# Alternating the two streams' rows in the last block, and issuing five weight splits earlier in the first

## The chip, the cores and the metric

The kernel runs on one core of one Trainium2 chip. The metric is the device time of one execution in microseconds. Engines are named as in the profile: PE is TensorE (matmuls), PEld its weight loads, DVE is VectorE, ACT ScalarE, POOL GpSimd, SP the engine that issues most DMAs.

## The reference

Two layers of a streaming encoder, applied to a prompt of 2048 frames and to a sample of 32 frames, each with its own conditioning vector and (for the sample) its own caches.

```python
h = rms_norm(x, norm_g) * (1.0 + scale) + shift          # scale, shift, gate from c @ w_ada + b_ada
# layer 0
q, k, v, g_a, u, g_s = split(h @ w_in_even)
o_a = sink_attention(rope(q), rope(k), v)                # 64-frame chunks, 2 chunks back
o_s = ssm_branch(u)                                      # complex diagonal recurrence, gelu, GLU
x = x + gate * (concat(o_a * silu(g_a), o_s * silu(g_s)) @ w_out_even)
# layer 1
b_g, c_g, hv, g_c = split(h @ w_in_odd)
x = x + gate * ((silu(g_c) * b_g * short_conv(c_g * hv)) @ w_out_odd)
y = rms_norm(x, final_g)
```

Returned are y of both, the new keys and values, the recurrence's last state and the last rows of the convolution's input. Everything is float32.

## The kernel before

Features lie on the 128 partitions, frames along the free axis; a row k (0 to 7) is one group of 128 of the 1024 features. The prompt is done in four blocks of 512 frames. The sample is a second stream, which goes along with the prompt in block 4 only: `streams_of(b)` gives `[(prompt, b)]` for blocks 1 to 3 and `[(prompt, 4), (sample, 1)]` for the last. Every engine runs its own hand-written program (`run_block`), in order, and the engines meet at counting semaphores, one for each kind of event of a stream: `S.wait(engine, block, event, k)` waits for the k-th such event.

A float32 product is made of three matmuls on parts: each activation and each weight is split into a rounded high part and the rest. `project` (L768) is one 1024 x 128 projection: for each row k, hi x hi, hi x lo, lo x hi. In the last block the two streams stand side by side in `hh_wide` and `hl_wide` (32 + 512 columns), and a row is 6 matmuls of 272 columns on each weight chunk (L789). With `ready`, `project` waits at row k for that row's event of every stream. It is called so for the pair c0, hv0 (event `h1`) and for the pair out1_0, out1_1 (event `g1`).

The activations' parts are made so:
- Norm 1, ahead of c0: PE puts the inverse roots into a bank (L822). DVE's `scale` (L1590) writes x times the root and a weight for row k into one of two buffers (L1598). ACT's `shift` (L1106) adds a bias and rounds (the high part, L1116). DVE makes the low part of row k-1 (L1604) in the same call of `scale`. `scale` needs the low part of row k-2, whose buffer it overwrites.
- Ahead of out1: POOL makes the last gated row (L1427), ACT's `round_mixed` rounds (L1130), DVE's `split_mixed` (L1627) subtracts (L1631).
- Norm 2, at the end: DVE's `output` (L1609) writes a row of y (L1612). When all eight rows of the prompt are there SP stores them, then the sample's, then ten small outputs.

The weights' parts are made in block 1 only, and stored for the later blocks, which load both parts with one DMA. In block 1 SP loads a raw chunk into a ring of two (L590), ACT rounds it into its slot of five (`split_hi`, L504, instruction L514), POOL subtracts (`split_lo`, L516, instruction L523), SP stores both. `load_raw(n)` waits until chunk n-2 is split, and `split_hi` until the slot's former chunk has been used and stored. Projections run in the order k, v, q0, q1, (transposes of u, the recurrence's input products x), q2, q3, ga0 to ga3, y (which takes four pairs loaded from `ssm_scratch`, L616), scores, gs0.

In block 1 the engines do between q0 and ga3, in this order:
- ACT: round q0 and q1; `swap` q0 and q1 (L1139, four copies that exchange halves for the rotary embedding); round q2, q3, ga0, ga1; swap q2; round ga2; swap q3; round ga3.
- DVE: `cos_part` of q0 and q1 (L1650, each waits for its swap); copy the transposed u (uT, L1782); products of x with cos and sin (L1663); `recurrence` (small adds L1677, two scans L1680, then products and h, L1684 to L1692); `cos_part` of q2 and q3.
- POOL: low halves of q0 and q1; sums of the input products (L1370, L1372); low halves of q2 and q3; two products of the scans (L1380, L1381); low half of ga0; h (L1390, L1394); low half of ga1; `rotate` q0 (L1351, L1354), `rotate` q1, low half of ga2, `rotate` q2, low half of ga3, `rotate` q3. The swap of q2 waits for the rotation of q0, the swap of q3 for that of q1.

Of the kernel before, what the change touches and what calls it, by code (L numbers as in the profile page):

```python
# [15 lines left out]
KT = D // P  # L16
# [32 lines left out]
SPLIT = [c for c in DENSE if not c.startswith("glu")]  # L49
# [248 lines left out]
def encoder(nc, vec, bc, d_skip, consts, mask, rope, xs, w_ada, w_dense, caches, outs):  # L298
    y_out, k_out, v_out, hre_out, him_out, conv_out = outs
    ctx = ExitStack()  # L300
    with ctx:
# [742 lines left out]
        def _(act):  # L1044
# [134 lines left out]
            def run_block(blk, streams, last=False):  # L1179
# [18 lines left out]
                for i in range(2):  # L1198
                    for S, b in streams(blk):
                        swap(S, b, f"q{i}", 1 + i)  # L1200
                for name, i in (("q2", None), ("q3", None), ("ga0", None), ("ga1", 2), ("ga2", 3), ("ga3", None)):
                    hi(name)
                    for S, b in streams(blk):
                        if i:
                            swap(S, b, f"q{i}", 1 + i)
# [59 lines left out]
                for S, b in streams(blk):  # L1265
                    shift(S, b, 1)
# [23 lines left out]
                for S, b in streams(blk):  # L1290
                    for k in range(KT):
                        round_mixed(S, b, 1, k)
# [25 lines left out]
        def _(pool):  # L1318
# [37 lines left out]
            def run_block(blk, streams, last=False):  # L1356
# [6 lines left out]
                lo("q0")  # L1363
                lo("q1")
# [9 lines left out]
                lo("q2")  # L1374
                lo("q3")
                for S, b in streams(blk):
# [6 lines left out]
                    if S.prompt:  # L1383
                        lo("ga0")
                        if blk == 1:
                            pool.wait_ge(split, SPLIT.index("ga0") + 1)
# [9 lines left out]
                lo("ga1")  # L1396
# [57 lines left out]
        def _(dve):  # L1454
# [160 lines left out]
            def norms(streams, l):  # L1615
                for S, b in streams:
                    mean(S, b, l)
                for S, b in streams:
                    diagonal(S, b, l)
                for S, b in streams:  # L1620
                    for k in range(KT + 1):
                        if l < 2:
                            scale(S, b, l, k)
                        elif k < KT:
                            output(S, b, k)

            def split_mixed(S, b, l, ks):  # L1627

                for k in ks:
                    S.wait(dve, b, f"g_hi{l}", k + 1)  # L1630
                    dve.tensor_tensor(S.hl[:, k, :], S.g[:, k, :], S.hh[:, k, :].bitcast(F32), ALU.subtract)\  # L1631
                        .then_inc(S.sem[f"g{l}"], 1)
# [124 lines left out]
            def run_block(blk, streams, last=False):  # L1757
# [124 lines left out]
                for S, b in streams(blk):  # L1882
                    split_mixed(S, b, 1, range(8))
# [144 lines left out]
```

## Time and profile before

| | us |
|---|---|
| median of 3 runs | 2185.78 (2183.31 to 2186.01) |
| the profiled execution | 2184.55 |
| its span | 2182.8 |
| PE busy | 2053.6 (94%) |
| PEld busy | 1638.3 (75%) |
| DVE busy | 801.2 (37%) |
| ACT busy | 496.6 (23%) |
| POOL busy | 442.2 (20%) |
| mean granted clock of TensorE | 0.958 of full speed |

Busy times are sums over the engine's instructions in one profiled execution. The span runs from its first to its last instruction. The chain that ended last tells which of them set the end; a wait is idle time of an engine just before an instruction, put down to what released it. Block 1 lies from about 130 to 640 us, the last block from about 1600 to the end.

### The profile page before, as it was taken

Reading aid. Unit: us, or ns where it says so; the run is one execution under the profiler, and the core shown is the slowest. Engines: PE = TensorE matmul, PEld = TensorE weight load, DVE = VectorE, ACT = ScalarE, POOL = GpSimd, SP = SyncE. Lnnn points to the kernel's source line nnn. Section 1 sums busy time; section 2 is a strip of 40 time slices with the busy share of each in tenths; the row PEclk is TensorE's granted clock in tenths of the full one; section 3 lists DMA queues with packets and bytes.
Section 4 is the critical chain, followed back from the end, with each engine's and each line's share of the span. In section 5 each row is a group of like instructions: output and inputs, shape, how many; then the busy total and the mean of one; then the engine's idle time right before and its main releaser. Section 6 shows DMA issues by size and latency. Waiting matters only on the chain.

```text
span 2182.8 us, 27958 instructions
## 1 busy us (share of the span) xinstructions
PE 2053.6 (94%) x11418; PEld 1638.3 (75%) x11434; DVE 801.2 (37%) x1502; ACT 496.6 (23%) x1047; POOL 442.2 (20%) x312
## 2 busy tenths in 40 slices
PE   8887899899999999999999999999999999799986
PEld 2256666688888857788887757888799876699986
DVE  7535272423443551312235543212425162322222
ACT  1232343322221431100121531000211442200010
POOL 0024514455431301001114001010104100100001
PEclk9988999999999999999999999999998999899998
DMA  8886735697778524555466414655474321345432
GB/s 283 309 240 231 263 152 172 242 316 273 259 291 264 188 87 173 193 189 188 175 198 243 173 62 169 233 191 187 156 235 148 127 78 69 125 155 175 176 145 72
DMA packets 86275, 415.00 MB, mean 190 GB/s; under 512 B 12404, under 2 KB 13460, under 8 KB 51892
## 3 DMA queue, kind: packets, MB, share of 16 engines
q1 hardware_dynamic: 79360, 396.37, 51.3%
q10 hardware_dynamic: 6788, 16.84, 2.6%
q8 instruction: 91, 1.49, 0.3%
q14 instruction: 36, 0.29, 0.0%
HBM read 323.51 MB, written 86.33 MB: 188 GB/s over the span
## 4 chain that ended last, share of the span: by engine, by line
PE 87%; DVE 4%; DMA 3%; POOL 2%; issue 2%; ACT 1%; SPq 0%; DVEq 0%; ACTq 0%; POOLq 0%
PE banks L762 17%; PE banks L760 17%; PE banks L761 17%; PE banks L789 16%; PE banks L1004 5%; PE banks L704 3%; PE banks L962 1%; PE banks L943 1%; PE banks L963 1%; PE banks L881 1%; PE banks L839 1%; DMA ring<-in_ada 1%; PE banks L869 1%; PE banks L812 1%; PE banks L822 1%
## 5 line engine op out<-in xcount | busy, mean ns | idle before, releaser
L760 PE MATMUL banks<-hh,pair 128*128 128x512 f32 x1464 | 584.5, 399 | 24.9 <-POOL pair L523 14.5
L762 PE MATMUL banks<-hh,pair 128*128 128x512 f32 x1464 | 584.8, 399 | 0.0
L761 PE MATMUL banks<-hl,pair 128*128 128x512 f32 x1464 | 577.4, 394 | 0.0
L789 PE MATMUL banks<-hh,pair 128*128 128x272 f32 x1952 | 332.9, 292 | 28.9 <-DVE hl L1604 12.7
L760 PEld LDWEIGHTS banks<-hh,pair 128*128 128x128 f32 x1464 | 278.8, 190 | 100.4 <-POOL pair L523 16.6
L761 PEld LDWEIGHTS banks<-hl,pair 128*128 128x128 f32 x1464 | 278.8, 190 | 68.0 <-issue 1.4
L762 PEld LDWEIGHTS banks<-hh,pair 128*128 128x128 f32 x1464 | 278.5, 190 | 61.5
L789 PEld LDWEIGHTS banks<-hh,pair 128*128 128x128 f32 x1952 | 282.4, 193 | 30.4 <-DVE hl L1604 12.8
L789 PE MATMUL banks<-hl,pair 128*128 128x272 f32 x976 | 205.1, 292 | 0.0
L523 POOL TENSOR_TENSOR pair<-ring,pair 128x1024 fp32r<-128x1024 f32 x62 | 152.8, 2467 | 209.2 <-ACT pair L514 209.2
L1339 POOL TENSOR_TENSOR pp_mem<-pp_mem 128x512 f32<-128x512 f32 x48 | 62.1, 1294 | 578.0 <-ACT pp_mem L1104 578.0
L789 PEld LDWEIGHTS banks<-hl,pair 128*128 128x128 f32 x976 | 156.8, 192 | 0.0
L1427 POOL TENSOR_TENSOR p_g<-p_t,pp_mem 128x512 f32<-128x512 f32 x32 | 41.8, 1307 | 551.1 <-DVE p_t L1878 551.1
L1753 DVE SCALAR_TENSOR_TENSOR p_x<-banks,mod,p_x 128x512 f32<-128x512 f32 x64 | 47.4, 750 | 269.6 <-PE banks L762 185.8
L1854 DVE TENSOR_TENSOR pp_mem<-p_sw,banks 128x512 f32<-128x512 f32 x32 | 22.0, 688 | 312.5 <-PE banks L762 223.3
L1004 PE MATMUL banks<-p_uT,pair 128*128 128x512 f32 x256 | 113.4, 602 | 0.0
L1104 ACT ACTIVATE pp_mem<-p_x 128x512 f32<-128x512 f32 x64 | 40.4, 632 | 285.6 <-DVE p_x L1753 285.2
L1139 ACT ACTIVATE p_sw<-banks 32x512 f32<-32x512 f32 x80 | 47.1, 589 | 221.5 <-POOL p_ut L1354 136.7
L760 PE MATMUL banks<-pair,hh 128*128 128x512 f32 (+1 forms) x272 | 93.6, 344 | 2.1 <-DVE hl L1604 2.1
L1004 PEld LDWEIGHTS banks<-p_uT,pair 128*128 128x128 f32 x256 | 48.3, 192 | 59.6 <-issue 54.5
L762 PE MATMUL banks<-pair,hl 128*128 128x512 f32 (+1 forms) x272 | 92.2, 339 | 0.0
L761 PE MATMUL banks<-pair,hh 128*128 128x512 f32 (+1 forms) x272 | 91.9, 338 | 0.0
(294 smaller groups left out, 2300.2 us busy)
## 6 DMA issues: line engine op xcount, KB each, us to landing
pair<-parts_scratch SPq DMA_DIRECT2D x198, 1024.0 KB, 4.8
parts_scratch<-pair SPq DMA_DIRECT2D x66, 1024.0 KB, 7.7
ring<-in_dense SPq DMA_DIRECT2D x62, 512.0 KB, 5.2
pair<-ssm_scratch SPq DMA_DIRECT2D x24, 1024.0 KB, 7.5
ring<-in_ada SPq DMA_DIRECT2D x24, 512.0 KB, 4.7
p_H<-in_ada SPq DMA_DIRECT2D x24, 512.0 KB, 4.7
p_x<-in_x SPq DMA_DIRECT2D x4, 2048.0 KB, 24.7
pair<-glu_scratch SPq DMA_DIRECT2D x8, 1024.0 KB, 5.0
```

The costliest lines, as they stand in the source:

```text
L523: pool.tensor_tensor(lo, raw(n), hi.bitcast(F32), ALU.subtract).then_inc(split, 1)
L704: mm = pe.matmul(psum[2 + j % 2][0:2, :], c_in[:, 2 * (i % 4) + k, :], ada_slots[i % NADASLOT][:, 512 * k:512 * k + 512], start=(i % 4 == ...
L760: pe.matmul(o, ah, bh, start=first, stop=False)
L761: pe.matmul(o, ah, bl, start=False, stop=False)
L762: return pe.matmul(o, al, bh, start=False, stop=last)
L789: mm = pe.matmul(o[n][:, WAT + WCOLS * half:WAT + WCOLS * (half + 1)], x, h[:, k, WCOLS * half:WCOLS * (half + 1)], start=(k == 0 and step ...
L1004: mm = pe.matmul(o, w[:, k, part * P:(part + 1) * P], S.yT[:, k, :], start=(k == 0), stop=(k == 3))
L1104: act.activation(sq[:, k % 2, :], x[:, k, :], ACT.Square).then_inc(S.sem[f"squared{l}"], 1)
L1139: ins = act.activation(S.sw[to:to + 32, n % 2, :], o[fr:fr + 32, 0:S.N], ACT.Copy)
L1339: pool.tensor_tensor(total, before, sq[:, k % 2, :], ALU.add).then_inc(S.sem[f"summed{l}"], 1)
L1427: pool.tensor_tensor(S.g[:, i, :], S.t1[:, i % 2, :], S.yc[:, i % 2, :], ALU.mult)\
L1753: dve.scalar_tensor_tensor(out=S.x[:, i, :], in0=o[:, 0:S.N], scalar=mod[:, l, 16 + i, S.index:S.index + 1], in1=S.x[:, i, :], op0=ALU.mul ...
```

## The change

Three loops over streams are turned inside out for norm 1 and for out1 (ACT and DVE), and with them DVE's loop of norm 2, which is the same function. Where only one stream runs, the order of instructions stays. In block 1 ACT rounds q2 and q3 between the swaps of q0 and q1. POOL makes the low halves of q2, q3 and ga0 right behind q1's, and that of ga1 behind the input sums. POOL's wait for its own split of ga0 goes. No instruction is added or taken away beside that wait; in blocks 2 to 4 the split calls do nothing.

```diff
@@ scalar, run_block
-                for i in range(2):
-                    for S, b in streams(blk):
-                        swap(S, b, f"q{i}", 1 + i)
-                for name, i in (("q2", None), ("q3", None), ("ga0", None), ("ga1", 2), ("ga2", 3), ("ga3", None)):
+                for S, b in streams(blk):
+                    swap(S, b, "q0", 1)
+                hi("q2")
+                hi("q3")
+                for S, b in streams(blk):
+                    swap(S, b, "q1", 2)
+                for name, i in (("ga0", None), ("ga1", 2), ("ga2", 3), ("ga3", None)):
...
-                for S, b in streams(blk):
-                    shift(S, b, 1)
+                for k in range(KT):
+                    for S, b in streams(blk):
+                        shift(S, b, 1, (k,))
...
-                for S, b in streams(blk):
-                    for k in range(KT):
+                for k in range(KT):
+                    for S, b in streams(blk):
                         round_mixed(S, b, 1, k)
@@ gpsimd, run_block
-                lo("q0")
-                lo("q1")
+                for name in ("q0", "q1", "q2", "q3", "ga0"):
+                    lo(name)
...
-                lo("q2")
-                lo("q3")
+                lo("ga1")
...
-                    if S.prompt:
-                        lo("ga0")
-                        if blk == 1:
-                            pool.wait_ge(split, SPLIT.index("ga0") + 1)
...
-                lo("ga1")
@@ vector, norms
-                for S, b in streams:
-                    for k in range(KT + 1):
+                for k in range(KT + 1):
+                    for S, b in streams:
                         if l < 2:
                             scale(S, b, l, k)
@@ vector, run_block
-                for S, b in streams(blk):
-                    split_mixed(S, b, 1, range(8))
+                for k in range(KT):
+                    for S, b in streams(blk):
+                        split_mixed(S, b, 1, (k,))
```

## Rows read from the trace of the kernel before

**Rows 1.** The page's chain that ended last, shares of the span by engine
```profile
PE 87%; DVE 4%; DMA 3%; POOL 2%; issue 2%; ACT 1%; SPq 0%; DVEq 0%; ACTq 0%; POOLq 0%
```

**Rows 2.** PE's waits, whole span: waiting line, releaser, us in total, times, longest
```profile
PE banks L760 <- POOL pair L523: 14.5, 4, 7.5
PE banks L789 <- DVE hl L1604: 12.7, 1, 12.7
...
PE banks L789 <- DVE hl L1631: 7.0, 1, 7.0
...
PE banks L962 <- DMA pair<-ssm_scratch: 3.7, 2, 2.4
```

**Rows 3.** Timeline of DVE, norm 1, last block: start, us, instruction, [idle before, releaser]
```profile
1896.31 0.75 DVE L1598 SCALAR_TENSOR_TENSOR pp_mem<-p_x,gscale,banks 128x512 f32<-128x512 f32 x1
1896.97 0.75 DVE L1604 SCALAR_TENSOR_TENSOR hl<-pp_mem,mod,hh 128x512 fp32r<-128x512 f32 x1
...
1906.76 0.25 DVE L1604 SCALAR_TENSOR_TENSOR hl<-s_im,mod,hh 128x32 fp32r<-128x32 f32 x1 [0.29 <-ACT hh L1116]
```

**Rows 4.** Timeline of DVE, norm 2 (the outputs of both streams)
```profile
2166.28 5.36 DVE L1612 SCALAR_TENSOR_TENSOR p_g<-p_x,vecs,banks 128x512 f32<-128x512 f32 x8 [2.14 <-PE banks L822]
2171.55 1.35 DVE L1612 SCALAR_TENSOR_TENSOR s_g<-s_x,vecs,banks 128x32 f32<-128x32 f32 x8
```

**Rows 5.** Timeline of PE, c0 and hv0; between these rows lie 20 more matmuls
```profile
1907.12 0.79 PE L789 MATMUL banks<-hh,pair 128*128 128x272 f32 x2 [12.74 <-DVE hl L1604]
...
1912.24 0.79 PE L789 MATMUL banks<-hh,pair 128*128 128x272 f32 x4
```

**Rows 6.** The chain in order of time, out1 stage: start, us, what
```profile
2108.82 50.55 PE banks L789 x384
```

**Rows 7.** Timelines of DVE and of POOL ahead of out1
```profile
2102.57 6.04 DVE L1631 TENSOR_TENSOR hl<-p_g,hh 128x512 fp32r<-128x512 f32 x8
...
2102.61 1.78 POOL L1427 TENSOR_TENSOR p_g<-p_t,pp_mem 128x512 f32<-128x512 f32 x1 [22.50 <-DVE p_t L1878]
```

**Rows 8.** The page's group of POOL's gated product: busy us, mean ns, idle before
```profile
L1427 POOL TENSOR_TENSOR p_g<-p_t,pp_mem 128x512 f32<-128x512 f32 x32 | 41.8, 1307 | 551.1 <-DVE p_t L1878 551.1
```

**Rows 9.** Busy time by stretch; behind POOL: PEclk, DMA share, GB/s
```profile
2104.00:2108.00 4.00, 0.00 (x0) 0.00 (x0) 4.00 (x7) 3.13 (x13) 1.06 (x2) 0.88 0.46 193
...
220.00:225.00 5.00, 4.15 (x18) 3.43 (x19) 4.16 (x2) 0.00 (x0) 4.84 (x3) 1.00 0.66 180
```

**Rows 10.** Timeline of ACT, block 1: the swap of q1, the roundings of q2 and q3
```profile
184.38 2.39 ACT L1139 ACTIVATE p_sw<-banks 32x512 f32<-32x512 f32 x4 [3.12 <-PE banks L762]
186.79 1.06 ACT L514 ACTIVATE pair<-ring 128x1024 fp32r<-128x1024 f32 x1
188.43 1.06 ACT L514 ACTIVATE pair<-ring 128x1024 fp32r<-128x1024 f32 x1 [0.58 <-DMA ring<-in_dense]
```

**Rows 11.** Timeline of PE, block 1: x, first matmul of ga2, y, scores
```profile
190.08 6.42 PE L943 MATMUL banks<-p_uT,pair 128*64 128x64 f32 x128 [3.60 <-issue]
...
237.92 0.50 PE L760 MATMUL banks<-hh,pair 128*128 128x512 f32 x1 [1.24 <-POOL pair L523]
...
249.17 0.43 PE L962 MATMUL banks<-pair,p_uT 128*64 128x128 f32 x2
...
267.57 0.81 PE L853 MATMUL banks<-mask_k,mask_q 128*128 128x512 bf16 x3 [0.16 <-issue]
```

**Rows 12.** Timelines of POOL and DVE, block 1: last input sum, small add, rotation
```profile
200.39 1.26 POOL L1372 TENSOR_TENSOR p_ut<-p_ut 128x512 f32<-128x512 f32 x1
...
202.12 1.88 DVE L1677 TENSOR_TENSOR work<-work,p_first 128x16 f32<-128x16 f32 x1 [2.87 <-POOL p_ut L1372]
...
229.21 1.28 POOL L1351 TENSOR_TENSOR p_sw<-p_sw,p_rope 128x512 f32<-128x512 f32 x1
```

**Rows 13.** Timeline of POOL, block 2: the scan's first product, the rotation of q0
```profile
706.27 3.45 POOL L1380 TENSOR_TENSOR pp_mem<-p_ut,cos_t 128x1024 f32<-128x1024 f32 x1 [4.97 <-DVE p_ut L1680]
...
720.03 1.29 POOL L1351 TENSOR_TENSOR p_sw<-p_sw,p_rope 128x512 f32<-128x512 f32 x1
```

## Prediction

> **What bounds the kernel now.** I read the chain that ended last first: PE is 87% of it [rows 1]. So an edit is worth what it takes from PE's waits, and nothing else. Then PE's waits, longest first [rows 2]. Four of them lie where the diff is. In the first block four projections wait for GpSimd's low halves (14.5 us), two state-space chunks for their transfers (3.7 us). In the last block there is one wait of 12.7 us ahead of the pair c0, hv0, ended by VectorE's split at L1604, and one of 7.0 us ahead of out1_0, out1_1, ended by L1631. Blocks 2 and 3 hold one stream and make no weight splits, so the diff changes nothing in them.
>
> **Last block, norm 1 (c0, hv0).** PE takes row k of both streams, in order. VectorE now finishes all prompt rows before the first sample row, so PE can start only after the sample's first split: 1906.76 plus 0.25, and PE starts 0.11 later, at 1907.12 [rows 3, 5]. With the rows alternating, prompt row 0 is split as before: its L1604 ends 0.10 before 1896.31, and so starts at 1895.45. The next instruction follows 0.66 behind a prompt one (1896.31 to 1896.97) [rows 3], and 0.16 behind a sample one: the eight sample outputs at the end take 1.35 us, so seven steps and the last one's 0.2 us [rows 4]. The sample's scale of row 1 then starts at 1896.11, its split of row 0 at 1896.27, which ends at 1896.52, and PE starts at 1896.63. That is **10.5 us sooner**.
> Does PE then run dry? A row of both streams costs VectorE 2 x 0.66 + 2 x 0.16 = 1.64 us; ScalarE's two shifts lie beside it. PE's 12 matmuls of a row cost 2.8 us at 1.2 GHz: the 22 from 1907.12 to 1912.24 took 5.12 us, 0.233 each [rows 5]. At 2.4 GHz they cost 1.5 us: the 384 of the out1 stage took 50.55 us, of which 22 are slow, which leaves 0.1255 each [rows 6]. PE begins slow in both kernels, is two rows behind when the clock rises, and is not caught up: row 7 is split by about 1908, and PE comes to it at 1909.4. So the whole shift is kept. If a switch between the streams costs 0.1 us more each (the 0.10 us that a prompt split now leaves before the next scale), row 7 comes at 1909.5 and 10.3 us stay. Cover that is gone: none, VectorE does the same instructions.
>
> **Last block, out1.** ScalarE's roundings and VectorE's splits alternate. Now eight prompt splits run from 2102.57 for 6.04 us before the first sample split [rows 7]; PE starts at 2108.82 [rows 6]. After the change the sample's first split is second in line, at 2103.3. GpSimd is then at the product of L1427, which here took 1.78 us from 2102.61 and so ended at 2104.39 [rows 7], against 1.31 us in the mean [rows 8]: it was held back, and these VectorE splits beside it too. I let the sample's split wait for its end, add 0.15 and 0.1 us, and get PE's start at 2104.6: **4.2 us sooner**. Without the waiting it would be 5.3, with the sample's product of GpSimd let through first 3.8.
> The Trainium skill (SBUF — State Buffer, "Who interferes with whom") says that a VectorE instruction with two SBUF inputs contends with a GpSimd instruction that reads SBUF, and that the later one blocks fully. Leaving it aside, the out1 shift would be the 5.3 us of free engines; the rows side with the rule.
> There is a second gain. PE's gap shrinks from 7.0 us to 2.8. In this gap the clock fell to 1.2 GHz only after 2104 (mean 0.88 from 2104 to 2108), and a gap of about 3 us ahead of 220.85 left it at 1.00 [rows 9]. So I take it that the clock stays up, which saves 22 x (0.233 - 0.1255) = **2.4 us**. Each later row is split 0.9 us after the last, faster than PE's 1.5.
>
> **Last block, norm 2.** The outputs alternate too. The prompt's eight take 5.36 us and the sample's 1.35 [rows 4]. The prompt's last one comes 7 x 0.16 = 1.1 us later, the sample's when it came before. The store of the prompt's y has to be issued first (0.6 us), then the sample's, then the ten small outputs, so the queue's tail moves by about **0.5 us, a loss**. Bounds: 0 and 1.1.
>
> **First block.** Three edits act together. ScalarE puts the rounding of q2 and q3 ahead of the swap of q1. GpSimd does the low halves of q2, q3 and ga0 ahead of the input products (L1370, L1372), and ga1's ahead of the wait for the scan.
> *The hold.* The swap of q1 now starts at 184.38, and the copy of q3 runs at 188.43 only, when its raw weights land (it waited 0.58 us for them) [rows 10]. Nothing that the diff touches is ahead of that transfer. Queued behind the copy, the swap starts at 189.43: 5.05 us later. Behind the swap wait VectorE's cosine product of q1, the copies of uT, and through them PE's x matmuls, at 190.08 now [rows 11], 195.1 then. q2, q3 and ga0 are ready by then and run without a gap after x: 4 projections at 5.6 us (ga2 and ga3 took 249.17 - 237.92) [rows 11] from 201.6, so ga1 ends at 224.
> *The recurrence.* GpSimd's input products now end at 201.65, then 206.7. There the low half of ga1 follows, 2.35 us, and blocks VectorE's first small add, as q2's does now (1.88 us for 16 columns) [rows 12]: 209.05. But q3's low half no longer blocks the scan. Block 2 has this stretch without splits: 4.97 us from the end of the products to L1380 at 706.27, and 13.76 on to the rotation of q0 at 720.03 [rows 13]. Some 0.3 us of the former are covered. That gives 213.7 and **227.5 for the rotation, against 229.21 now** [rows 12]. The hold (5.05) and ga1's block (2.4) eat most of what the splits gave back.
> *What follows.* Swap of q2, rounding of ga2 and its low half follow the rotation in the same order. ga2 starts at 236.2 instead of 237.92 [rows 11], after 12 us of idle PE, so at 1.2 GHz (2.4 us). y would start at 236.2 + 11.25 + 2.4 = 249.85, against 249.17. Its 18.4 us to the scores (267.57) held 3.7 us of waits for transfers [rows 2, 11]. SP's raw load of ga3 waits for ga1's low half, and behind it in SP's order stand the store of ga0, the x load and the first two state-space loads. That half is done at 209 instead of just ahead of the rotation at 229.21 [rows 12]. So those transfers are out of the queue before the last two state-space loads, and y runs in 14.7: the scores start at 264.55. **Gain 3.0 us**, from waits for transfers that go, not from the splits themselves. Bounds: -0.7 with the transfers as late as now, 5.4 with ga2 at full clock. Further down the first block PE waits for no low half, and everything behind moves with it.
>
> **Sum.** 10.5 + 4.2 + 2.4 - 0.5 + 3.0 = 19.6 us. The profiled execution took 2184.55 us (span 2182.8), and would take 2164.95. The median of the three runs shown is 2185.78, 1.2 above it, so the median comes to **2166.2 us**.
>
> **Rivals.**
> 1. *The clock falls in the short gap before out1.* It falls at some time after PE goes idle, and 2.8 us is close. Against: the gap ahead of 220.85. Price 2.4 us: 2168.6. Chance 0.14. The Trainium skill (TensorE: Matmul & The Clock Gate, "What's actually happening") has the throttled level as the default, and activity as what lifts it; that fits rows 5 and 9 and sets no price.
> 2. *The first block gives nothing*: the state-space loads stay in the way, because the larger ones are served no sooner. 2166.2 + 3.7 = 2169.9. For: the queue is the one shared by all. Chance 0.12.
> 3. *The swap of q1 is not held*: q3's weights land early, and the x chain keeps its place: 5 us more, 2161.2. Against: the landing at 188.43. Chance 0.06.
> 4. *PE stays at 1.2 GHz while it takes c0 and hv0 row by row*: eight rows at 2.8 us from 1896.6 end at 1919.0 where now they end at 1921.6 (22 slow and 74 fast). 2.6 us instead of 10.5: 2174.1. Against: rows come every 1.64 us, so PE has no gap. Chance 0.06.
> 5. *The alternation frees nothing*, because something else ends PE's wait: only 3.0 us are left, 2182.8. Against: PE starts 0.11 us after the sample's first split [rows 3, 5]. Chance 0.04.
> 6. *Slower: the hold grows.* ScalarE is stuck at the rounding of q3 until its weights land, and each us after 188.43 moves swap, x, scan and all behind by one. Slower than before from 19.6 us later, slower by 0.2% from 24 us later, say 2190.5. Against: 0.58 us of waiting now. Chance 0.02.
>
> **Numbers.** Forecast 0.56. The range 2159 to 2174 takes in rivals 1 to 3, the bounds of each term, and touches rival 4. A measurement of this kernel can tell about 0.2% (4.4 us) from no change. Faster 0.94 (forecast and rivals 1 to 4), same 0.04 (rival 5), slower 0.02.
>
> **What would show it.** PE's first matmul of c0 about 10 us nearer to the norm's rows, starting slow. A gap before out1 under 3 us and a first matmul at full clock. In the first block a longer gap before x (8.6 us), no gap before q2, ga0 and ga1, a gap of 12 us before ga2, none in y. Wrong would be: no longer gap before x, a gap inside the c0, hv0 pair, or the same waits for pair<-ssm_scratch.

## The result, and the profile after

| | before | after |
|---|---|---|
| median, us | 2184.55 (2182.71 to 2186.01, 4 runs) | 2165.85 (2161.48 to 2166.35, 4 runs) |
| ratio after to before | | 0.9916 [0.9903, 0.9929] |
| the profiled execution, us | 2184.55 | 2166.01 |
| its span, us | 2182.8 | 2164.2 |
| PE busy, us | 2053.6 | 2050.0 |
| mean granted clock | 0.958 | 0.960 |

The changed kernel is 18.7 us faster, where a median of 2166.2 us was forecast. The page of after shows the chain that ended last, which answers to [rows 1]:

```profile
PE 89%; DVE 4%; issue 2%; POOL 2%; DMA 2%; ACT 1%; SPq 0%; DVEq 0%; ACTq 0%; POOLq 0%
```

PE's waits in after, to be laid beside [rows 2] (waiting line, releaser, us in total, times, longest):

```profile
PE banks L943 <- issue: 15.9, 4, 8.2
...
PE banks L760 <- POOL pair L523: 12.9, 1, 12.9
...
PE banks L789 <- issue: 2.7, 1, 2.7
...
PE banks L789 <- DVE hl L1602: 2.2, 1, 2.2
```

The two waits of the last block, 12.7 and 7.0 us, are now 2.2 and 2.7. The four waits for GpSimd's low halves have become one of 12.9 us. The waits for pair<-ssm_scratch are gone. The first block's x matmuls (L943) now wait 8.2 us, where they waited 3.6.

**Where the 18.6 us of the span went.** Two stretches of the program have nothing to do with the diff and still differ from execution to execution, so I cut the span at marks inside it and compare the pieces. The marks are ScalarE's swap of k (L1139, first row that ACT has in block 1 behind the projections of k), VectorE's first maximum over the scores (TENSOR_REDUCE), the root's matmuls of a norm (L822), and PE's first matmul of c0 and of out1 (L789).

| stretch | before | after | change | forecast |
|---|---|---|---|---|
| start of the span to swap of k | 162.61 | 161.41 | -1.20 | 0 |
| swap of k to the first maximum of block 1 | 106.86 | 102.18 | -4.68 | -3.0 |
| to the root of norm 1, last block | 1622.30 | 1623.02 | +0.72 | 0 |
| to c0 | 15.35 | 4.86 | -10.49 | -10.5 |
| to out1 | 201.70 | 197.50 | -4.20 | -4.2 |
| out1 to the last norm's L812 | 52.04 | 52.49 | +0.45 | -2.4 |
| to that norm's root | 3.34 | 3.22 | -0.12 | 0 |
| to the end of the span | 18.60 | 19.52 | +0.92 | +0.5 |
| sum | | | -18.60 | -19.6 |

The sum is within 1.0 us of the forecast, but not every line is. The clock's gain did not come, the first block gave 1.7 us more, the tail cost 0.4 us more, and 1.2 us are the start, which the diff doesn't touch: it lay between 158.8 and 163.8 us in the thirteen profiles of this document. Two single executions can therefore differ by up to 5 us for a reason that has nothing to do with the change.

**Norm 1.** Timeline of DVE in after, answering to [rows 3]: start, us, instruction.

```profile
1890.29 0.75 DVE L1602 SCALAR_TENSOR_TENSOR hl<-pp_mem,mod,hh 128x512 fp32r<-128x512 f32 x1
1890.96 0.24 DVE L1596 SCALAR_TENSOR_TENSOR s_im<-s_x,gscale,banks 128x32 f32<-128x32 f32 x1
1891.12 0.25 DVE L1602 SCALAR_TENSOR_TENSOR hl<-s_im,mod,hh 128x32 fp32r<-128x32 f32 x1
1891.28 0.74 DVE L1596 SCALAR_TENSOR_TENSOR pp_mem<-p_x,gscale,banks 128x512 f32<-128x512 f32 x1
...
1892.93 0.74 DVE L1596 SCALAR_TENSOR_TENSOR pp_mem<-p_x,gscale,banks 128x512 f32<-128x512 f32 x1
```

And PE's first matmul of c0, answering to [rows 5]:

```profile
1891.47 0.79 PE L789 MATMUL banks<-hh,pair 128*128 128x272 f32 x2 [2.25 <-DVE hl L1602]
```

The sample's first split is the second instruction behind the prompt's first; before it came behind all of the prompt's. PE starts 0.35 us after that split began, where it was 0.36 in the kernel before (1906.76 to 1907.12). Each row costs VectorE 1892.93 - 1891.28 = 1.65 us, against 1.64 forecast, and PE has no gap inside the pair.

**Out1.** Timelines of DVE, of POOL and of PE in after, answering to [rows 6, 7]:

```profile
2087.00 0.69 DVE L1629 TENSOR_TENSOR hl<-p_g,hh 128x512 fp32r<-128x512 f32 x1
2087.61 1.26 DVE L1629 TENSOR_TENSOR hl<-s_g,hh 128x32 fp32r<-128x32 f32 x1
...
2089.50 0.18 DVE L1629 TENSOR_TENSOR hl<-s_g,hh 128x32 fp32r<-128x32 f32 x1
```
```profile
2087.05 1.77 POOL L1425 TENSOR_TENSOR p_g<-p_t,pp_mem 128x512 f32<-128x512 f32 x1 [22.50 <-DVE p_t L1876]
```
```profile
2088.97 0.79 PE L789 MATMUL banks<-hh,pair 128*128 128x272 f32 x2 [2.73 <-issue]
```

The sample's first split has 32 columns. It takes 1.26 us where the later ones take 0.18: it lies under GpSimd's product and ends 0.05 us after it (2088.87, the product 2088.82). That was the assumption of the forecast, gap and all (2.8 forecast, 2.73 measured). GpSimd's product in turn is held back by the prompt's split ahead of it (1.77 us against 1.31 in the mean, [rows 8]).

PE's first two matmuls take 0.79 us, which is the slow clock. The busy time by stretch (columns as in [rows 9]) shows when it fell in after:

```profile
2086.00:2088.00 2.00, 0.24 (x2) 0.02 (x1) 1.72 (x4) 1.66 (x5) 0.95 (x1) 1.00 0.47 74
2088.00:2089.00 1.00, 0.03 (x1) 0.06 (x1) 1.00 (x2) 1.00 (x5) 1.00 (x2) 0.60 0.77 319
2089.00:2090.00 1.00, 1.00 (x4) 1.00 (x5) 1.00 (x3) 1.00 (x4) 0.03 (x1) 0.50 0.95 401
...
2094.00:2096.00 2.00, 2.00 (x14) 2.00 (x13) 0.00 (x0) 0.00 (x0) 0.00 (x0) 0.74 0.00 0
```

The granted clock is 1.00 to 2088, 0.60 in the next microsecond, and then 0.50 (1.2 GHz) until it rises between 2094 and 2096. PE had been idle since 2086.2. A mean of 0.60 over 2088 to 2089 puts the fall at about 2088.2 (0.2 us at 1.00 and 0.8 at 0.50).

**First block.** Timeline of ACT in after, answering to [rows 10]:

```profile
161.41 2.39 ACT L1139 ACTIVATE p_sw<-banks 32x512 f32<-32x512 f32 x4 [4.93 <-PE banks L762]
...
183.07 1.06 ACT L514 ACTIVATE pair<-ring 128x1024 fp32r<-128x1024 f32 x1 [3.02 <-DMA ring<-in_dense]
186.74 1.06 ACT L514 ACTIVATE pair<-ring 128x1024 fp32r<-128x1024 f32 x1 [2.61 <-DMA ring<-in_dense]
187.82 2.39 ACT L1139 ACTIVATE p_sw<-banks 32x512 f32<-32x512 f32 x4
```

And PE's rows, answering to [rows 11]: x, first matmul of ga2, first of y.

```profile
193.52 5.61 PE L943 MATMUL banks<-p_uT,pair 128*64 128x64 f32 x128 [8.25 <-issue]
...
234.34 0.80 PE L760 MATMUL banks<-hh,pair 128*128 128x512 f32 x1 [12.92 <-POOL pair L523]
...
247.34 0.43 PE L962 MATMUL banks<-pair,p_uT 128*64 128x128 f32 x2
```

Both roundings wait for their weights, the second until 186.74, 25.3 us behind the swap of k (before: 188.43 - 162.61 = 25.8). The swap of q1 stands behind them. Between x and ga2, and between ga2 and the scores, PE has no wait.

### The profile page after: what moved, and what is told of

The parts are those of the page before. It is cut to its first block, busy times and chain, and to the rows that moved or that the text cites. A ratio compares the mean times of both kernels' runs of the same rounds, so it can differ in the third digit from the quotient of the medians.

```text
span 2164.2 us, 27973 instructions
## 1 busy us (share of the span) xinstructions
PE 2050.0 (95%) x11434; PEld 1636.8 (76%) x11434; DVE 800.2 (37%) x1502; ACT 496.4 (23%) x1047; POOL 441.2 (20%) x312
## 4 chain that ended last, share of the span: by engine, by line
PE 89%; DVE 4%; issue 2%; POOL 2%; DMA 2%; ACT 1%; SPq 0%; DVEq 0%; ACTq 0%; POOLq 0%
PE banks L762 18%; PE banks L760 18%; PE banks L761 17%; PE banks L789 16%; PE banks L1004 6%; PE banks L704 3%; PE banks L962 2%; PE banks L963 2%; DMA ring<-in_ada 1%; PE banks L943 1%; PE banks L881 1%; PE banks L839 1%; PE banks L869 1%; PE banks L812 1%; PE banks L822 1%
## 5 line engine op out<-in xcount | busy, mean ns | idle before, releaser
L760 PE MATMUL banks<-hh,pair 128*128 128x512 f32 x1464 | 583.6, 399 | 23.3 <-POOL pair L523 12.9
L762 PE MATMUL banks<-hh,pair 128*128 128x512 f32 x1464 | 584.3, 399 | 0.0
L760 PEld LDWEIGHTS banks<-hh,pair 128*128 128x128 f32 x1464 | 278.5, 190 | 97.3 <-POOL pair L523 13.7
L789 PE MATMUL banks<-hh,pair 128*128 128x272 f32 x1952 | 333.5, 293 | 14.2 <-DVE s_t L1648 5.7
L762 PEld LDWEIGHTS banks<-hh,pair 128*128 128x128 f32 x1464 | 278.3, 190 | 61.6
L789 PEld LDWEIGHTS banks<-hh,pair 128*128 128x128 f32 x1952 | 283.0, 193 | 15.6 <-issue 13.2
L789 PE MATMUL banks<-hl,pair 128*128 128x272 f32 x976 | 205.1, 292 | 0.0
L789 PEld LDWEIGHTS banks<-hl,pair 128*128 128x128 f32 x976 | 157.1, 193 | 0.0
L1139 ACT ACTIVATE p_sw<-banks 32x512 f32<-32x512 f32 x80 | 47.1, 589 | 229.7 <-POOL p_ut L1358 147.9
L760 PE MATMUL banks<-pair,hh 128*128 128x512 f32 (+1 forms) x272 | 93.4, 343 | 2.1 <-DVE hl L1602 2.1
L762 PE MATMUL banks<-pair,hl 128*128 128x512 f32 (+1 forms) x272 | 91.9, 338 | 0.0
```

Of the source, the lines that this page charges most:

```text
L760: pe.matmul(o, ah, bh, start=first, stop=False)
L762: return pe.matmul(o, al, bh, start=False, stop=last)
L789: mm = pe.matmul(o[n][:, WAT + WCOLS * half:WAT + WCOLS * (half + 1)], x, h[:, k, WCOLS * half:WCOLS * (half + 1)], start=(k == 0 and step ...
L1139: ins = act.activation(S.sw[to:to + 32, n % 2, :], o[fr:fr + 32, 0:S.N], ACT.Copy)
```

## Experiments

All ratios are to the kernel before, run on the same chip beside the experiment, with a 95% interval. "First maximum" is the time from the swap of k to the first maximum over the scores (106.86 us before, 102.18 after); "out1 to norm" the time from PE's first matmul of out1 to the last norm's L812 (52.04 and 52.49). Beside the three groups of experiments (e1 to e4, e5 to e8, e9 to e11) the kernel before took 2182.31, 2182.39 and 2183.94 us in the median, not 2184.55; so ratios and marks are to be compared, and the times in the expectations are up to 2.2 us high by that alone.

### Each half of the change alone

e1_last_only takes the first block's order back:

```diff
-                for S, b in streams(blk):
-                    swap(S, b, "q0", 1)
-                hi("q2")
-                hi("q3")
-                for S, b in streams(blk):
-                    swap(S, b, "q1", 2)
+                for i in range(2):
+                    for S, b in streams(blk):
+                        swap(S, b, f"q{i}", 1 + i)
...
-                for name in ("q0", "q1", "q2", "q3", "ga0"):
-                    lo(name)
+                lo("q0")
+                lo("q1")
```

> The last block's alternation alone; the first block as in the kernel before. Theory (the gains lie in separate places and add up): norm 1 gives 10.5 us, out1 4.2 us without any clock gain, the output's tail costs 0.5 to 0.9: some 14 us less than before, about 2170.5, and c0 starts 4.9 us after the norm's root matmul instead of 15.4. Rival (the clock stays up in the short gap ahead of out1 when it lies elsewhere in time): 2.4 us more, 2168. Rival (PE's slow start eats the shift): 2178.

e2_first_only takes the alternation back:

```diff
-                for k in range(KT):
-                    for S, b in streams(blk):
-                        shift(S, b, 1, (k,))
+                for S, b in streams(blk):
+                    shift(S, b, 1)
...
-                for k in range(KT + 1):
-                    for S, b in streams:
+                for S, b in streams:
+                    for k in range(KT + 1):
```

> The first block's order alone; the last block as in the kernel before. Theory: 3 to 5 us less than before (about 2180), with the copy of q3 holding the swap of q1, PE's gap before x above 8 us, a gap of 12 to 13 us ahead of ga2, none in y. Rival (the first block gives nothing, all of the change is the last block's): 2184.5. Rival (the two parts work on each other, so that both alone do not add up to the whole): their sum differs from 18.7 us by more than 3.

Measured: e1 2166.58 us (2166.08 to 2166.89), ratio 0.9929 [0.9912, 0.9945]. First maximum 106.72, so the first block is as before; gap ahead of c0 2.25 us, ahead of out1 2.73, tail 19.5. e2 2177.62 us (2174.22 to 2181.31), ratio 0.9979 [0.997, 0.9988]. Gaps 12.75 and 7.00, as before; first maximum 103.97, 2.9 us less than before.

The halves gave 0.71% and 0.21%, together 0.92%, and the whole gave 0.84%. The intervals are 0.18% to 0.33% wide, so the halves add up as far as this can tell. Three quarters of the gain is the alternation. Of the first block's half I can say only that it is a gain of some 3 to 5 us: it showed 2.9 us in this profile, and 4.2 to 5.1 in those of after, e4, e5, e9 and e11, which have the same first block. Most of the spread lies in one transfer. ScalarE's rounding of q3 starts 25.0 to 26.2 us behind the swap of k in these six profiles, latest in e2, and x starts 6.8 us behind that rounding in each (31.8 to 33.0). The rest of e2's is 0.7 us of slow clock: it takes 13.72 us from ga2 to y, where after takes 13.00. So a mark of one profile can't tell less than about 2 us in the first block.

### The hold: swap of q1 ahead of the roundings

```diff
-                hi("q2")
-                hi("q3")
                 for S, b in streams(blk):
                     swap(S, b, "q1", 2)
+                hi("q2")
+                hi("q3")
```

> The changed kernel, but ScalarE swaps q1 before it rounds q2 and q3, as in the kernel before. Theory (the hold of the swap by q3's raw weights costs the x chain 5 us, and all up to ga2 hangs on it): PE's gap before x back at 3.6 us, x 3 to 5 us sooner, ga2 and the scores 3 to 4 us sooner, about 2162. Rival (the hold is hidden, since ga2's start is set by the splits and transfers, not by x): the same time as the changed kernel, 2165.9. Rival (the low halves now fall later and stand in front of GpSimd's input sums): slower, up to 2168.

Measured: 2162.19 us (2161.14 to 2163.93), ratio 0.9909 [0.9895, 0.9924]; first maximum 99.25, 2.9 us less than after. PE's timeline, x:

```profile
189.71 6.40 PE L943 MATMUL banks<-p_uT,pair 128*64 128x64 f32 x128 [3.61 <-issue]
```

x starts 27.5 us behind the swap of k, as before (27.5), where after has 32.1. The wait of 8.2 us ahead of x is the hold: it is back at 3.6 once the swap no longer stands behind the rounding of q3. Of its 4.6 us, 2.9 arrive at the scores; ahead of ga2 PE then waits 13.75 us instead of 12.92. So this part of the change is worth undoing. The intervals of e3 and of after overlap, so the 2.9 us rest on the marks within the profile, not on the medians. The six profiles with the first block of after have 101.8 to 104.0 us to the first maximum, so e3's 99.25 is 2.5 to 4.7 below them.

### Low half of ga1 behind the scan's products

```diff
-                lo("ga1")
                 for S, b in streams(blk):
...
                                        ALU.add).then_inc(S.sem["h_im"], 1)
+                lo("ga1")
```

> The changed kernel, but ga1's low half stays behind h, as in the kernel before. Theory (ga1's early low half takes as much from the scan as it gives back to the rotation; what it buys is that the transfers behind it in SP's order leave early, and y runs without a wait): the scan is done 2.4 us sooner, the rotation starts where it did, and y has its waits for the state-space loads again, 2 to 3.7 us: about 2169. Rival (y's waits went with the other edits): the same time as the changed kernel, 2165.9.

Measured: 2167.45 us (2166.13 to 2171.09), ratio 0.9937 [0.9913, 0.9961]; first maximum 105.44, 3.3 us more than after. The intervals of the two ratios overlap. PE's timeline, ga1, ga2 and y:

```profile
224.75 0.80 PE L760 MATMUL banks<-hh,pair 128*128 128x512 f32 x1 [9.42 <-POOL pair L523]
...
233.39 0.50 PE L760 MATMUL banks<-hh,pair 128*128 128x512 f32 x1 [0.39 <-POOL pair L523]
...
254.43 0.66 PE L962 MATMUL banks<-pair,p_uT 128*64 128x128 f32 x2 [2.59 <-DMA pair<-ssm_scratch]
```

The queue of SP, in e8 and then in after: the raw load that waits for ga1's low half, and the x load behind it.

```profile
224.73 0.33 SPq L590 DMA_DIRECT2D ring<-in_dense  x1
...
225.58 0.60 SPq L620 DMA_DIRECT2D p_x<-in_x  x1
```
```profile
207.32 0.33 SPq L590 DMA_DIRECT2D ring<-in_dense  x1
...
208.17 0.60 SPq L620 DMA_DIRECT2D p_x<-in_x  x1
```

This is the run that tells the theory of the first block from its rival. With the low half late, the wait for pair<-ssm_scratch in y comes back (2.6 us), and the first matmuls behind it run slow. From the first matmul of y to the first maximum e8 takes 20.49 us; the kernel before takes 20.30 and e1 20.36, which have the low half late too, and the seven profiles with it early and ga2 and ga3 in their place (after, e2, e3, e4, e5, e9, e11) take 16.25 or 16.26. This stretch hardly varies, so the 4.2 us are firm; y itself starts 1.0 us sooner in e8 than in after, which leaves 3.3. In e8 the raw load is issued 65.05 us behind the swap of k, in after 45.91 us. The rotation of q0 comes at 64.98 us in e8 and at 64.29 in after, so for GpSimd's own order the early split is worth only 0.7 us: what it buys is the transfers behind it in SP's queue.

### Outputs of norm 2 one stream after the other

```diff
-                for k in range(KT + 1):
+                for k in range(KT + 1 if l < 2 else 0):
                     for S, b in streams:
-                        if l < 2:
-                            scale(S, b, l, k)
-                        elif k < KT:
-                            output(S, b, k)
+                        scale(S, b, l, k)
+                for S, b in streams if l == 2 else []:
+                    for k in range(KT):
+                        output(S, b, k)
```

> The changed kernel, but the outputs of norm 2 run one stream after the other. Theory (the alternated outputs delay the prompt's store and the queue of stores behind it): from the last norm's root matmul to the end 18.6 us as before instead of 19.5, so 0.9 us less. Rival (the tail is set by the sample's store, which comes when it came before): at most 0.2 us.

Measured, in one run: 2161.6 us, span 2159.8. From the root to the end of the span 18.55 us, where after took 19.52. The first two stores and the last of all on SP's queue, in e4 and in after:

```profile
2148.71 0.59 SPq L632 DMA_DIRECT2D y<-p_g  x1
2149.98 0.34 SPq L632 DMA_DIRECT2D y<-s_g  x1
...
2157.91 0.43 SPq L688 DMA_DIRECT2D hi<-s_last  x1
```
```profile
2153.26 0.59 SPq L632 DMA_DIRECT2D y<-p_g  x1
2153.90 0.66 SPq L632 DMA_DIRECT2D y<-s_g  x1
...
2162.32 0.43 SPq L688 DMA_DIRECT2D hi<-s_last  x1
```

Reckoned from the root (2141.25 and 2144.68), the store of the sample's y comes at 8.73 in e4 and at 9.22 in after: 0.49 us later, the half microsecond that was forecast. The last store comes at 16.66 and at 17.64: 0.98 later. The other half is in the issue times of the queue, above all the sample's y, 0.66 us against 0.34. The other profiles agree: from the root to the end the five with plain outputs (before, e2, e4, e7, e10) take 18.52 to 18.60 us, the eight with alternating ones 19.10 to 19.54. So the alternation costs 0.5 to 1.0 us at the end and gives nothing there, since no matmul waits for these outputs.

### Low halves of ga2 and ga3 earlier

```diff
-                for name, i in (("ga0", None), ("ga1", 2), ("ga2", 3), ("ga3", None)):
+                for name in ("ga0", "ga1", "ga2", "ga3"):
                     hi(name)
+                for i in (2, 3):
                     for S, b in streams(blk):
-                        if i:
-                            swap(S, b, f"q{i}", 1 + i)
+                        swap(S, b, f"q{i}", 1 + i)
...
                 lo("ga1")
+                lo("ga2")
```

> The changed kernel, but ScalarE rounds ga2 and ga3 ahead of the swaps of q2 and q3, and GpSimd makes ga2's low half behind ga1's and ga3's ahead of the rotations. Theory (PE's 12.9 us ahead of ga2 are only the place of its split behind the rotation of q0; y needs the rotations, but ga2 and ga3 don't): the gap ahead of ga2 goes, a smaller one comes ahead of or inside y, since h and the rotations are 4 to 5 us later by two low halves; 5 to 8 us less than the changed kernel, about 2159. Rival (y is bound by the recurrence and the rotations, so the gap only moves): 2165.9. Rival (the low half of ga2 in front of the scan waits for its raw weights, behind the 2 MB copy of the gate weights): slower, 2168.

The low half of ga3 stands ahead of the rotations. Measured: 2159.25 us (2155.78 to 2161.94), ratio 0.9893 [0.9871, 0.9915]; first maximum 97.41, 4.8 us less than after and 4.4 to 6.6 less than the six profiles with its first block. The intervals of the two ratios still overlap. PE's timeline:

```profile
232.27 0.50 PE L760 MATMUL banks<-hh,pair 128*128 128x512 f32 x1 [3.17 <-POOL pair L523]
245.56 0.40 PE L962 MATMUL banks<-pair,p_uT 128*64 128x128 f32 x2 [2.28 <-DVE p_g L1698]
```

The wait of 12.9 us ahead of ga2 is gone. In its place stand 3.2 us ahead of ga3 and 2.3 us in y, where PE has now caught up with VectorE's own products. This matmul after the gap of 3.17 us took 0.50 us, so it ran at full clock. But the clock fell right behind it: the granted clock is 0.90 from 232 to 233 and 0.50 from 233 to 236.

### Who goes first ahead of out1

e5_sample_first puts the sample's row ahead of the prompt's, in ScalarE's roundings and in VectorE's splits alike:

```diff
                 for k in range(KT):
-                    for S, b in streams(blk):
+                    for S, b in streams(blk)[::-1]:
                         split_mixed(S, b, 1, (k,))
```

> The changed kernel, but ahead of out1 ScalarE and VectorE take the sample's row k before the prompt's. Theory (with the prompt's split first, GpSimd's product takes the engines' turn in between and the sample's small split waits 1.3 us for it; the gap is what a full split and that wait make): the gap ahead of out1 shrinks from 2.73 us to about 1.5 to 1.8, as the prompt's split is let in before GpSimd's product, and the clock is up at out1's first matmul. Rival (GpSimd's product simply comes first and the prompt's split waits instead): the gap stays at 2.5 or more.

Measured, in one run: 2160.1 us, span 2158.3, gap ahead of out1 2.67 us. Timelines of DVE and POOL in e5:

```profile
2082.61 0.18 DVE L1629 TENSOR_TENSOR hl<-s_g,hh 128x32 fp32r<-128x32 f32 x1
2082.71 1.78 DVE L1629 TENSOR_TENSOR hl<-p_g,hh 128x512 fp32r<-128x512 f32 x1
```
```profile
2082.67 1.26 POOL L1425 TENSOR_TENSOR p_g<-p_t,pp_mem 128x512 f32<-128x512 f32 x1 [22.60 <-DVE p_t L1876]
```

I had thought that the small split, once out of the way, would leave the prompt's split free. GpSimd's product now starts 0.04 us ahead of the prompt's split and the split pays: 1.78 us instead of 0.69. The gap is shorter by 0.06 us only. One of the two big instructions must stand behind the other, whichever is first.

e9_sample_product_first turns GpSimd's order instead, so that its last gated product of the sample comes before that of the prompt:

```diff
-                    for S, b in streams(blk):
+                    for S, b in streams(blk)[::-1 if i == KT - 1 else 1]:
                         S.wait(pool, b, "gate_b", i + 1)
```

> The changed kernel, but GpSimd makes the sample's last gated product before the prompt's. Theory (GpSimd's 1.3 us product of the prompt gets in between VectorE's two first splits and holds the sample's; with the sample's small product in its place only 0.25 us stand there): the gap ahead of out1 goes from 2.73 us to about 1.8. On the clock: if the fall to 1.2 GHz in the changed kernel is the gap's doing, it stays up at 1.8 us and the stage's 384 matmuls take about 48.5 us instead of 49.8 to 51.0, 2 to 3 us less in all. Rival (any such gap makes it fall): 49.8 or more, 1 us less. Rival (GpSimd's product gets in first anyway): no change.

Measured: 2161.79 us (2158.64 to 2165.29), ratio 0.9893 [0.9877, 0.991]; gap 1.71 us, out1 to norm 50.15 us. Timelines of DVE, POOL and PE in e9:

```profile
2090.26 0.24 DVE L1629 TENSOR_TENSOR hl<-s_g,hh 128x32 fp32r<-128x32 f32 x1
...
2091.03 1.30 DVE L1629 TENSOR_TENSOR hl<-s_g,hh 128x32 fp32r<-128x32 f32 x1
```
```profile
2089.79 0.66 POOL L1425 TENSOR_TENSOR s_g<-s_t,s_wk 128x32 f32<-128x32 f32 x1 [22.59 <-DVE s_t L1876]
2090.42 1.86 POOL L1425 TENSOR_TENSOR p_g<-p_t,pp_mem 128x512 f32<-128x512 f32 x1
```
```profile
2090.60 0.49 PE L789 MATMUL banks<-hh,pair 128*128 128x272 f32 x2 [1.71 <-DVE hl L1629]
```

The long hold has moved from the split of row 0 to that of row 1, where PE still has row 0 to do. And the clock stays up. Against after, the gap gives 1.02 us and the stage behind it 2.34; the intervals of the two ratios overlap, so this too rests on the marks. Busy time by stretch in e9:

```profile
2091.00:2092.00 1.00, 1.00 (x10) 1.00 (x9) 1.00 (x2) 1.00 (x4) 1.00 (x1) 1.00 1.10 467
2092.00:2094.00 2.00, 1.87 (x15) 1.68 (x14) 2.00 (x6) 2.00 (x7) 0.28 (x1) 1.00 0.47 197
```

### Out1 without the alternation

e11_out1_plain is after, with ScalarE's roundings and VectorE's splits ahead of out1 one stream after the other:

```diff
-                for k in range(KT):
-                    for S, b in streams(blk):
-                        split_mixed(S, b, 1, (k,))
+                for S, b in streams(blk):
+                    split_mixed(S, b, 1, range(8))
```

> The changed kernel without the alternation ahead of out1; norm 1 and norm 2 still alternate. Theory (out1's alternation is worth the shorter gap alone, since the clock falls either way): gap 7.0 us again, the stage's 384 matmuls 49.7 to 50.6, 3.7 to 4.5 us more than the changed kernel, about 2170. Rival (the forecast's term, with 2.4 us for a clock that stays up): 6.6 us more, 2172.4.

Measured: 2169.3 us (2167.29 to 2172.82), ratio 0.9934 [0.9919, 0.9949]; gap 7.00 us, out1 to norm 51.61 us. That is 3.5 us above after, and 0.18% in the ratios, whose intervals overlap. The marks are sharper: the gap is 4.27 us longer, the stage behind it 0.88 us shorter, and a clock that stays up in after's gap would have shown as 2.4 us on top of the gap. So the alternation ahead of out1 brings the shorter gap and nothing from the clock.

### Versions put together

e7_all has the edits of e3, e6, e4 and e5 together; e10_all_product_first those of e3, e6, e4 and e9.

> All together: swap of q1 first, ga2 and ga3 early, sample first ahead of out1, outputs one stream after the other. Theory (the four touch separate waits): 3.5 + 6 + 0.9 + 1.5 us less than the changed kernel, about 2154. Rival (swap first and early splits share one wait, the recurrence): 2158.

> Swap of q1 first, ga2 and ga3 early, outputs one stream after the other, and the sample's last gated product first on GpSimd. Theory: the same as with all together before, 2153.7, or 1 to 2 us less through the shorter gap ahead of out1. Rival (the shorter gap gives nothing): 2154.

Measured: e7 2153.7 us (2151.92 to 2154.39), ratio 0.9867 [0.9848, 0.9886], first maximum 91.71, gap 2.67, out1 to norm 52.51. e10 2150.58 us (2148.61 to 2152.03), ratio 0.9846 [0.9831, 0.9861], first maximum 91.82, gap 1.71, out1 to norm 50.23. The first block of these two is 10.4 us shorter than that of after; e3 gave 2.9 of it and e6 4.8 by themselves, so some 2.7 us come only with both, as far as single profiles can tell that differ by 2 us with the same first block. e10 is 3.1 us below e7; in the profiles the gap gives 0.96 of it and the stage behind it 2.28. The intervals of e7 and e10 just overlap; both lie clear of that of after. It is the fastest version here, 15.3 us below after in the medians. Its PE waits, where after has 15.9 and 12.9:

```profile
PE banks L943 <- issue: 11.3, 4, 3.6
...
PE banks L760 <- POOL pair L523: 4.2, 1, 4.2
```

## Why the prediction was right, and where it was not

**Norm 1: right.** 10.49 us against 10.5. It was the term with a row for each of its parts: a prompt instruction's 0.66, a sample one's 0.16, PE's 0.11 behind the split. Rival 4 (PE limps at 1.2 GHz row by row) and rival 5 (the alternation frees nothing) are refuted by c0 to out1: 201.70 us before and 197.50 after, and the whole change of 4.20 is the gap ahead of out1, so nothing of the shift was given back inside.

**Out1, the gap: right, and for the reason given.** 4.27 us against 4.2. The sample's split waited for GpSimd's product, as taken: 1.26 us for 32 columns. e9 turned that product's order, and the gap fell from 2.73 to 1.71. The Trainium skill (SBUF — State Buffer, "Who interferes with whom") has the two engines share a pair of ports under an exclusive lock; the rows of after, e5 and e9 agree, with 1.26, 1.78 and 1.30 us on whichever instruction of VectorE came second.

**Out1, the clock: wrong.** The step that failed is "So I take it that the clock stays up". It rested on one stretch, a gap of about 3 us at 220.85 with the clock at 1.00 up to 225, and rival 1 with a chance of 0.14 is what happened. The clock fell at about 2088.2, with PE idle since 2086.2, and the stage took 52.49 us instead of the 49.6 that were forecast. The trace of the kernel before already had a case against the step, the next gap of the same kind in the first block. PE waited 2.66 us there, its first matmul still ran at full clock, and then the clock fell (timeline of PE; busy time by stretch):

```profile
229.30 0.50 PE L760 MATMUL banks<-hh,pair 128*128 128x512 f32 x1 [2.66 <-POOL pair L523]
...
230.00:232.00 2.00, 2.00 (x6) 1.62 (x5) 0.00 (x0) 0.06 (x1) 1.92 (x3) 0.50 0.88 172
```

e11 shows that the gap of 7.00 us and that of 2.73 pay about the same: 51.61 and 51.3 to 52.5. e9 and e10, with 1.71 us, pay nothing: 50.15 and 50.23. The size was off too: from a stage behind the gap of 7.0 us (52.04 before, 51.20 in e2, 51.61 in e11) to one in which the clock stays up (50.15, 50.23) there are 1.0 to 1.9 us to be had, not 2.4. The sign that the prediction named, a first matmul at full clock, would not have told either: e1, e4, e5, e6 and e8 show it, and their clock fell all the same.

**Norm 2: right in sign and mechanism, the size about twice the forecast.** A loss of 0.92 us against 0.5. The sample's store comes 0.49 us later, as worked out from the queue of two stores; the other half microsecond is in the queue's own issue times, which the sum took as fixed.

**First block: right in what happens, 1.7 us off in size.** Each step, from the swap of k:

| step | forecast | measured |
|---|---|---|
| x later (the hold) | 5.05 | 4.64 |
| rotation of q0 | 64.9 | 64.29 |
| ga2 sooner | 1.7 | 2.38 |
| ga2, ga3 longer by the slow clock | 2.4 | 1.75 |
| y to the first maximum shorter | 3.7 | 4.05 |
| sum | 3.0 | 4.68 |

The steps were off by 0.35 to 0.7 us each, all to the same side (the first two are contained in the third). The last one is the firmest, since it comes out the same in seven profiles; the others moved by about 1 us between profiles with the same first block, so that the 4.68 of this profile stands for 2.9 to 5.1. The mechanism stands: rival 3 (the swap is not held) is refuted by the 8.25 us ahead of x and by e3, rival 2 (the state-space loads stay in the way) by the wait that is gone and by e8, in which it comes back. ga2 ran slow for 13.00 - 11.25 = 1.75 us. The forecast took over the 2.4 us of the 22 slow matmuls ahead of out1; here the rows of L760 to L762 come 0.43 us apart up to 238 and 0.23 apart from then on, which is some 8 slow ones. The slower case, rival 6 (the hold grows), did not come: q3's weights landed 25.3 us behind the swap of k, not later than the 25.8 of before, and the first rounding too had to wait for its weights, 3.02 us.

**The sum.** For the profiled execution 2164.95 us was worked out and 2166.01 came. The main terms hold, but that the total is so near is luck, because errors cancel: the clock -2.9, the tail -0.4, the middle of the program -0.7, against the first block +1.7 and the start +1.2. That is 4.0 us in one direction and 3.0 in the other. The median came 0.35 us from the forecast, since the 1.2 us by which the earlier median of before stood above its profiled execution were gone as well. The range had to be as wide as it was.

**Open.** The fall of the clock isn't the same in two executions, and what decides it was not tried (below). Why the start of the span differs by up to 5 us between profiles is open too, and so is what makes the issues on SP's queue longer in after's tail than in e4's.

## What to carry to other kernels

Where a matmul takes its rows from two streams, split row by row across the streams, not stream by stream: PE can start after the first row of both instead of the last. Compare VectorE's cost of a row with PE's: at norm 1 it was 1.65 us against PE's 2.8 at 1.2 GHz and 1.5 at 2.4 GHz, and it cost nothing because PE began slow and so fell behind VectorE. A PE at full clock from the start would have waited some 0.15 us at each of seven rows, 1 us in all (an estimate from these costs; no run shows it). Do so only where a matmul waits (at norm 2 it cost 0.5 to 1.0 us), and when a weight split is moved, look at what the issuing queue holds behind it: here moving one low half was worth 3.3 us, and only 0.7 us of it on GpSimd itself; the rest came from the transfers behind it. Put no rounding that waits for a transfer ahead of work that is ready: that hold cost 2.9 us of the first block's gain.

## What the runs showed of the hardware

**The clock falls in a gap of 2.7 us, and not always at the same place.** In after the granted clock fell to 0.60 in the stretch from 2088 to 2089, with PE idle. e1 has the same last block and the same gap of 2.73 us, and there PE's first matmul still ran at full clock; the clock fell later, with PE at work:

```profile
2090.00:2091.00 1.00, 0.32 (x2) 0.35 (x3) 1.00 (x2) 1.00 (x4) 1.00 (x2) 1.00 0.99 418
2091.00:2092.00 1.00, 1.00 (x10) 1.00 (x9) 1.00 (x5) 1.00 (x5) 0.29 (x1) 0.98 0.97 410
2092.00:2094.00 2.00, 2.00 (x11) 2.00 (x10) 2.00 (x7) 1.28 (x5) 0.00 (x0) 0.50 0.08 33
```

The profiles fall into two groups. In after, e3 and e7 out1 begins slow, and out1 to norm takes 52.49, 52.51 and 52.51 us; in e1, e4, e5, e6 and e8 it begins at full clock and takes 51.32, 51.30, 51.43, 51.29 and 51.30. The gap is 2.67 to 2.73 in all eight. The first group also has the root's matmuls of norm 1 at 2.06 us, the second at 1.50 to 1.58, some 200 us earlier. after and e4 give every engine the same instructions in the same order up to the outputs of norm 2, and yet one is in the first group and one in the second. So it is the clock's timing against the program that differs, and not the code. e9 has 2.06 and e10 1.51 for that root, and both keep the clock with a gap of 1.71 us. The Trainium skill (TensorE: Matmul & The Clock Gate, "What's actually happening") says that the monitor behind the clock runs free and isn't reset by the kernel, so that the point of a change varies; the two groups agree. What a gap costs hangs on that timing, here by 1.2 us: from the start of out1 on PE works 6.1 us at 1.2 GHz in after, and 3.3 to 3.4 us in e1 and e4. One gap of 3 us without a fall, as the one ahead of 220.85 [rows 9], is therefore no proof that the next one is free: behind 2.66 us ahead of 229.30 in the same trace, and behind 3.17 us in e6, the clock fell within 0.6 us of PE's first matmul. Nor does the time since PE went idle settle it: the fall came 2.0 us after in after, and 5.2 us after ahead of out1 in the kernel before (idle from 2101.8, fall at 2107.0). Behind 2.3 us ahead of y it fell in e6 and not in e7 or e10.

**A small instruction waits out the big one ahead of it.** A split of 32 columns took 1.26 us instead of 0.18, and an add of 16 columns ahead of the scan 1.94 us instead of 0.18 (205.41 in after's timeline of DVE), because GpSimd had started first; in e5 it was 0.04 us that decided. Turning the two streams around on VectorE moved the hold and saved 0.06 us; turning them around on GpSimd saved 1.02.
